# Stick-breaking heads: the strict mask moves from a TensorE matmul to a VectorE minimum behind the exponential

## The reference

```python
z = jnp.einsum('bqhd,bkhd->bhqk', qb, k, preferred_element_type=jnp.float32) * scale
q_pos = i * BLOCK + jnp.arange(BLOCK)
before = key_pos[None, :] < q_pos[:, None]
log_1m_beta = jnp.where(before, jax.nn.log_sigmoid(-z), 0.0)
tail = lax.cumsum(log_1m_beta, axis=3, reverse=True) - log_1m_beta
a = jnp.where(before, jnp.exp(jax.nn.log_sigmoid(z) + tail), 0.0).astype(v.dtype)
return jnp.einsum('bhqk,bkhd->bqhd', a, v)
```

## Time and profile before

| | before |
|---|---|
| median of three runs | 1734.01 us (1733.11 to 1734.31) |
| the profiled execution | 1734.41 us |
| its span, first to last instruction | 1732.6 us |
| TensorE busy | 1704.3 us |
| VectorE busy | 1107.1 us |
| ScalarE busy | 854.7 us |
| GpSimd busy | 142.0 us |
| mean granted TensorE clock | 0.997 |

### The profile page before, as it was taken

One profiled execution on the slowest core, in us unless ns is written; L12 is line 12 of the kernel. 1 busy time (PEld: TensorE's weight loads), 2 busy tenths in 40 slices (PEclk: granted clock), 3 DMA queues, 4 the chain that ended last, 5 costly groups with the idle time before them and its releaser, 6 DMA issues.

```text
span 1732.6 us, 21793 instructions
## 1 busy us (share of the span) xinstructions
PE 1704.3 (98%) x8585; PEld 1437.6 (83%) x8585; DVE 1107.1 (64%) x1498; ACT 854.7 (49%) x1203; POOL 142.0 (8%) x140
## 2 busy tenths in 40 slices
PE   9999999999999999999999999999999999999997
PEld 6888888888898888888888888888888988888886
DVE  8887887775566534364587777877754665344545
ACT  7576666665355414131466755666644554232223
POOL 0111211111100000000001111111111000000000
PEclk9999999999999999999999999999999999999999
DMA  4121121222432222222321211122224122222222
GB/s 149 67 73 59 60 74 62 77 75 80 138 118 74 97 98 97 98 98 97 119 82 65 76 61 61 61 74 74 74 85 164 68 98 97 98 97 98 97 98 73
DMA packets 47495, 152.09 MB, mean 88 GB/s; under 512 B 5153, under 2 KB 9633, under 8 KB 47394
## 3 DMA queue, kind: packets, MB, share of 16 engines
q1 hardware_dynamic: 45664, 147.42, 24.5%
q10 hardware_dynamic: 1730, 3.28, 0.5%
HBM read 146.49 MB, written 4.19 MB: 87 GB/s over the span
## 4 chain that ended last, share of the span: by engine, by line
PE 83%; issue 7%; DVE 6%; ACT 3%; POOL 1%; DMA 1%; DVEq 0%; SPq 0%; ACTq 0%; POOLq 0%
PE bank L579 77%; PE bank L584 3%; PE bank L834 1%; PE bank L885 1%; POOL mix L2303 1%; ACT w_hi L1039 1%; DVE w_lo L1582 0%; DVE h_lo L1617 0%; DVE hf L1629 0%; PE bank L588 0%; DMA x<-in_x 0%; PE bank L687 0%; DVE x L1638 0%; DVE fb L1828 0%; ACT dn L1096 0%
## 5 line engine op out<-in xcount | busy, mean ns | idle before, releaser
L579 PE MATMUL bank<-h_hi,w_hi 128*128 128x512 f32 (+1 forms) x1224 | 477.7, 390 | 4.6 <-DVE h_lo L1617 2.4
L579 PE MATMUL bank<-h_hi,w_lo 128*128 128x512 f32 (+1 forms) x1224 | 472.3, 386 | 0.0
L579 PE MATMUL bank<-h_lo,w_hi 128*128 128x512 f32 (+1 forms) x1224 | 472.3, 386 | 0.0
L1039 ACT ACTIVATE w_hi<-raw 128x1024 fp32r<-128x1024 f32 (+2 forms) x269 | 271.0, 1013 | 220.0 <-DMA raw<-in_w 219.6
L1582 DVE TENSOR_TENSOR w_lo<-raw,w_hi 128x1024 fp32r<-128x1024 f32 (+2 forms) x269 | 316.8, 1181 | 63.3 <-ACT w_hi L1039 56.9
L579 PEld LDWEIGHTS bank<-h_hi,w_hi 128*128 128x128 f32 x1224 | 230.4, 188 | 54.8 <-issue 5.7
L579 PEld LDWEIGHTS bank<-h_hi,w_lo 128*128 128x128 f32 x1224 | 230.3, 188 | 46.9
L579 PEld LDWEIGHTS bank<-h_lo,w_hi 128*128 128x128 f32 x1224 | 230.5, 188 | 45.2 <-issue 1.7
L579 PE MATMUL bank<-u_hi,w_hi 128*128 128x512 f32 (+1 forms) x560 | 208.0, 371 | 0.0
L579 PE MATMUL bank<-u_hi,w_lo 128*128 128x512 f32 (+1 forms) x560 | 207.7, 371 | 0.0
L579 PE MATMUL bank<-u_lo,w_hi 128*128 128x512 f32 (+1 forms) x560 | 207.7, 371 | 0.0
(11 more groups left out here) (264 smaller groups left out, 2747.3 us busy)
## 6 DMA issues: line engine op xcount, KB each, us to landing
raw<-in_w SPq DMA_DIRECT2D x251, 512.0 KB, 3.2
x<-in_x SPq DMA_DIRECT2D x16, 256.0 KB, 3.3
side_raw<-in_w SPq DMA_DIRECT2D x6, 512.0 KB, 4.8
x_spill<-x ACTq DMA_DIRECT2D x8, 256.0 KB, 2.5
x<-x_spill SPq DMA_DIRECT2D x8, 256.0 KB, 3.2
out_y<-x SPq DMA_DIRECT2D x8, 256.0 KB, 2.1
raw<-in_w SPq DMA_DIRECT2D x8, 192.0 KB, 2.4
raw<-in_w SPq DMA_DIRECT2D x8, 128.0 KB, 2.3
```

The source lines that it names most:

```text
L579: mm = pe.matmul(o, s, m, start=start and i == 0 and j == 0, stop=last and i == n - 1 and j == 2, skip_group_check=True)
L1039: act.activation(chunk_in(gc, w_hi, side_hi)[:, 0:w], chunk_in(gc, raw, side_raw)[:, 0:w], ACT.Copy)\
```

## The change

TensorE no longer adds the mask in `stick_tail`; the last matmul of each piece releases the exponential. Behind the exponentials of a head VectorE takes, in two instructions of 128 x 256, the minimum of the four diagonal blocks with a new table `tri_most`, which is 2^127 where the mask holds and 0 elsewhere (`stick_masked`). `stick_probs_hi` waits for both. ScalarE's split of the chunk moves from behind `stick_probs_hi(h)` to ahead of it. `tri01` is now made from `tri_most` by a scale; GpSimd's wait for it is taken once a layer, not once a head.

```diff
-                    def masked(b):
-                        causal_mask(*stick[h % 2][b], b, MASK_STRICT).then_inc(tail_full.sem, 1)
-
...
-                    less(0, P, 3 * P, NEG_ONE, later[:, 0:3 * P])
-                    masked(0)
-                    less(1, P, 2 * P, NEG_ONE, later[:, 4 * P:6 * P])
-                    masked(1)
+                    less(0, P, 3 * P, NEG_ONE, later[:, 0:3 * P]).then_inc(tail_full.sem, 1)
+                    less(1, P, 2 * P, NEG_ONE, later[:, 4 * P:6 * P]).then_inc(tail_full.sem, 1)
                     if h % 2:
                         pe.wait_ge(*a_exp(3 * h))
                     own(3)
-                    less(2, P, P, NEG_ONE, later[:, 3 * P:4 * P])
-                    masked(2)
+                    less(2, P, P, NEG_ONE, later[:, 3 * P:4 * P]).then_inc(tail_full.sem, 1)
...
                 def stick_probs_hi(h):
                     act.wait_ge(*a_exp(3 * h + 3))
+                    act.wait_ge(*a_mask(2 * h + 2))
                     act.wait_ge(*pv_full(2 * HEADS + h))
...
-                act.activation(tri01[:, :], cst_f[:, TRI01 * P:(TRI01 + 1) * P], ACT.Copy).then_inc(const_set, 1)
+                act.activation(tri_most[:, :], cst_f[:, TRI_MOST * P:(TRI_MOST + 1) * P], ACT.Copy).then_inc(const_set, 1)
+                act.activation(tri01[:, :], cst_f[:, TRI_MOST * P:(TRI_MOST + 1) * P], ACT.Copy, scale=1.0 / MOST)\
+                    .then_inc(const_set, 1)
...
                         stick_probs(h)
+                        split((C["stick_vt", p + 1] if more else C["gate", 2, 2]) + 2)
                         stick_probs_hi(h)
-                        split((C["stick_vt", p + 1] if more else C["gate", 2, 2]) + 2)
...
+                def stick_masked(h):
+
+                    b = fb[h % 2]
+                    dve.wait_ge(const_set, 3)
+                    dve.wait_ge(*a_exp(3 * h + 3))
+                    most = tri_most[:, :].unsqueeze(1).broadcast_to([P, 2, P])
+                    for two in (b[:, 0:2 * SEQ].rearrange("p (a c) -> p a c", a=2)[:, :, 0:P],
+                                b[:, 7 * P:9 * P].rearrange("p (a c) -> p a c", a=2)):
+                        dve.tensor_tensor(two, two, most, ALU.min).then_inc(a_mask.sem, 1)
...
                         stick_lo(h + 1)
                         if p:
                             stick_out(p - 1)
+                        stick_masked(h)
                         if more:
                             stick_in_low(p + 1, 1)
                         probs_lo(2 * HEADS + h, fb[0][:, :], p_hi[:, :], p_lo[:, :])
...
                             split(C["gate", 2, 2] + 2)
                             gate_in(2, 2)
+                        stick_masked(h + 1)
                         stick_sum(h)
```

More of the change, by code:

```diff
@@ L121 @@
 VECS = V_SINK + HEADS
-IDENT, SWAP, NEG_TRI, NEG_ONE, ONE, MASK_CAUSAL, MASK_PREV, MASK_STRICT, NEG_PART, TRI01 = range(10)
-N_CONST = 10 * P
+IDENT, SWAP, NEG_TRI, NEG_ONE, ONE, MASK_CAUSAL, MASK_PREV, NEG_PART, TRI_MOST = range(9)
+N_CONST = 9 * P
 TRIG = 4 * 4
@@ L128 @@
 BIG = 1e30
+MOST = 2.0 ** 127
 TWO_PI = float(2 * np.pi)
@@ L143 @@
 CAUSAL_COLS, BANDED_COLS = 1280, 896
+DIAGONAL = (0, 512, 896, 1024)
 def side_by_side():
@@ L194, in sem @@
             return ctx.enter_context(nc.semaphore(name))
-        tri01 = place("tri01", [P, P], F32)
+        tri_most, tri01 = (place(n, [P, P], F32) for n in ("tri_most", "tri01"))
         vec_all = place("vec_all", [P, DEPTH * VECS + TRIG], F32)
@@ L206, in trunk @@
         tab = place("tab", [P, 4, SEQ], F32)
-        cst = place("cst", [P, 9, P], F32R)
+        cst = place("cst", [P, 8, P], F32R)
         rstd_x = place("rstd_x", [P, SEQ], F32)
@@ L421, in trunk @@
         a_exp = signal("a_exp", 24)
+        a_mask = signal("a_masked", 16)
         sbo_part = signal("sb_o_part", 8)
@@ L1295, in _ @@
                 act.wait_ge(warmed, 1)
-                act.activation(cst[:, :, :], cst_f[:, 0:9 * P].rearrange("p (a c) -> p a c", a=9), ACT.Copy)\
+                act.activation(cst[:, :, :], cst_f[:, 0:8 * P].rearrange("p (a c) -> p a c", a=8), ACT.Copy)\
                    .then_inc(const_set, 1)
-                act.activation(tri01[:, :], cst_f[:, TRI01 * P:(TRI01 + 1) * P], ACT.Copy).then_inc(const_set, 1)
+                act.activation(tri_most[:, :], cst_f[:, TRI_MOST * P:(TRI_MOST + 1) * P], ACT.Copy).then_inc(const_set, 1)
+                act.activation(tri01[:, :], cst_f[:, TRI_MOST * P:(TRI_MOST + 1) * P], ACT.Copy, scale=1.0 / MOST)\
+                    .then_inc(const_set, 1)
                 table_sin(2, QPE, 2, slice(HEAD, P))
@@ L2323, in _ @@
                         band_maximum(n)
+                    pool.wait_ge(const_set, 3)
                     for h in range(HEADS):
@@ L2328, in _ @@
                             mix_in(1, h - 1)
-                        pool.wait_ge(const_set, 2)
                         pool.wait_ge(*z_max(3 * h + 3))
-                        for off in (0, 512, 896, 1024):
+                        for off in DIAGONAL:
                             to = fb[h % 2][:, off:off + P]
@@ L2345, in constants @@
     mats = [p == c, swap == c, -(p >= c).astype(np.float32), -np.ones((P, P)), np.ones((P, P)),
-            -BIG * (p > c), -BIG * (p <= c), -BIG * (p >= c), np.full((P, P), -1.0 / P), p < c]
+            -BIG * (p > c), -BIG * (p <= c), np.full((P, P), -1.0 / P), MOST * (p < c)]
     const = np.concatenate([np.asarray(m, np.float32) for m in mats], axis=1)
```

## The result

The changed kernel took 1747.42 us in the median of four runs (1743.97 to 1749.84), beside 1733.59 us before (1733.11 to 1734.31): ratio 1.0077, 95% interval 1.0063 to 1.0092, slower by 13.8 us. The forecast was slower by 9.5 us, 1743.5, with a range of 1740.5 to 1749.5. The profiled execution took 1746.67 us with a span of 1744.9, 12.3 us more than the 1732.6 before.

A forecast was written before the change was run, and what follows sets the result against it. TensorE, busy 98% of the span, was taken as the bound, waiting for p_lo at stick_values(2p). Added waits of 4.75 us a layer, 9.5 in two, on the profiled 1734.41 gave 1743.9, or 1743.5 as a median; range 1740.5 to 1749.5.

The forecast's parts named there:

- part 3: At stick_values(2p), minimums queued behind stick_lo and stick_out delay p_hi, p_lo and the values: 4.75 us a layer, 9.5 in two.
- part 2: On VectorE, two added minimums a head take 0.42 us each, 0.76 us together with overlap; bounds 0.48 and 1.30.
- part 1: In TensorE's tails, 48 removed mask matmuls save 0.24 us a head, 3.8 us in all, waited away at stick_values(2p).
- part 4: ScalarE's split ahead of p_hi costs nothing; VectorE's extra 0.76 us before gate(1,2p+1) costs nothing, with 0.7 us of cover.
- The likeliest case: The whole kernel takes 1743.5 us with no fall of the clock; chance 0.60 within the size bounds.
- Rival (A): TensorE's clock falls behind the longer holes, 1.6 us each: two falls give 1746.7, all six 1753.1; chance 0.25.
- its own row at 9.2 us: TensorE did 0.07 us of work from 9.20 to 11.50 us; from 12.50 the granted clock is 0.52.
- (B): At stick_values(2p), VectorE is not in the way and TensorE keeps its 3.8 us: 1730.2 us; chance 0.05.
- (C): VectorE falls behind after p_lo, with minimums of 0.69 us and waits before gate(1,2p+1): 1750.2 us; chance 0.05.
- (D): On VectorE, minimums cost the floor, 0.28 less a pair, 2.2 us in all: 1741.3 us; included in the 0.60.

The follow-up runs named there:

- first: The kernel before without its 48 mask matmuls and with nothing in their place: 1733.48 us, ratio 0.9999.
- second: The kernel before with all mask matmuls kept, plus the minimums, their wait and the moved split: 1746.39 us, ratio 1.0071.
- third: The changed kernel with stick_masked(h) moved one instruction earlier on VectorE, ahead of stick_out(p-1): 1743.15 us, ratio 1.0055.
- fifth experiment: The changed kernel with ScalarE's split moved back behind p_hi: 1747.29 us, ratio 1.0090.

## Why the prediction was right or wrong

**The chain at stick_values (part 3): right.** Predicted were 1.08, 1.51, 1.50 and 0.66 us for the four pairs; measured 1.12, 1.57, 1.56 and 0.58, together 4.83 against 4.75. Adding the minimums with the masks kept, and moving them by one instruction, showed that their place is the cause.

**The minimums (part 2): right.** 418 ns in the median of 32 and 0.76 us for a pair of them, as taken from the row of 128 x 256. The prediction gave 0.84 us as the price by the Trainium skill, "VectorE: DVE Perf Modes", section "The DRAIN you can't avoid". That left out the section's exception, that an instruction which isn't held starts earlier; the trace shows such an overlap, 0.08 us in a pair.

**The masks (part 1): the saving was waited away, as said, but its size was wrong.** A tail went from 1.97 to 1.61 us, 0.36 a head, not 0.24. The step that failed is the pricing of each mask from its own start to the next. The loads of stationary weights show why. In the kernel before, tail of head 2 (start, us, engine):

```profile
303.40 0.19 PEld L584 LDWEIGHTS bank<-sp_lo,cst 128*128 128x128 f32 x1
303.52 0.19 PEld L584 LDWEIGHTS bank<-later,cst 128*128 128x128 f32 x1
303.64 0.19 PEld L584 LDWEIGHTS bank<-cst 128*128 128x128 f32 x1
303.75 0.19 PEld L579 LDWEIGHTS bank<-h_hi,w_hi 128*128 128x128 f32 x1
```

The first line is the load for a matmul of 256 columns, the second and third are for matmuls of 128. In this stretch the loads start 0.11 to 0.12 us apart whatever the width. A matmul of 128 columns can start 0.06 us ahead of the next, but three loads of 0.12 make 0.36, which is what the tail lost. That the loads are the cause is read from these rows; no run varied them. In this kernel the error changed mainly the length of the holes, 2.80 and 2.10 us where 2.6 and 2.0 were said.

**The split and the rest (part 4): right.** The split cost nothing in either place, and gate(1,2p+1) waited no longer than before. Not foreseen: in pair 0 the projection behind the first tail came early enough to wait 0.30 us for VectorE to empty its bank, inside the shadow of the hole:

```profile
259.42 0.47 PE L582 MATMUL bank<-h_hi,w_hi 128*128 128x512 f32 x1 [0.30 <-DVE tmp L1661]
```

**The likeliest case: wrong by the clock.** Rival (A) was named and priced, two falls of 1.6 us and 1746.7 us. It happened, at 1.6 and 1.5 us in the profile, and the median is 1747.42. The forecast took no fall as likeliest, at 0.60 against 0.25, though its own row at 9.2 us showed a fall behind a stop of 2.3 us, and two of the holes it predicted were longer than that and four nearly as long. The 1743.5 of part 3's sum is near the fastest run (1743.97) and the kernel with its holes filled (1743.49), so it is the time without falls. The median lay within the range because that left room for three falls; the chain alone would not have brought it to 1747.42, and one of the four runs (1749.84) is above the range.

**Rivals (B), (C) and (D)** did not come: no pair's values started straight behind the tail, no gate waited longer, and the minimums were not shorter than taken.

## What to carry to other kernels

Work taken from the busiest engine can be worth nothing until the next wait of that engine is moved too, as 48 matmuls were here: ask at which wait the saving arrives, and what has to be earlier there. When that wait is for another engine, an instruction added to the other engine costs what its place in the queue makes it cost, not only its length: 0.76 us of minimums cost 1.5 us a pair here. And before giving up an edit that only lengthened a wait, look for independent work that the waiting engine can do in it: one projection in front of the values turned a loss of 13.8 us into a gain of 9.1, of which 4.6 come without the change and 4.5 with it.

## What the runs showed of the hardware

TensorE's clock fell to 1.2 GHz behind waits shorter than I had reckoned with. In the stick heads of the profiles of the kernel before and of the five with longer holes (the changed kernel and the first, second, third and fifth experiment), a fall, to a granted clock of 0.50, stood behind 6 of 8 holes of 2.5 to 2.8 us, 2 of 8 of 2.1 us, 1 of 2 of 1.7 us, and none of the 8 of 1.4 to 1.5 us, the 2 of 1.34 us or any shorter one. The same hole of the same kernel had a fall in one layer and none in the other, for which I have no cause, and the changed kernel's time is spread over its runs by 5.9 us, against 0.5 us with the holes filled. Each fall cost 1.5 to 1.6 us. The Trainium skill, "TensorE: Matmul & The Clock Gate", section "HAM oscillation — how this bites in real kernels", describes such losses for waits for transfers; here the wait was for VectorE.

In a tail's short matmuls with changing weights, the loads start 0.11 to 0.12 us apart, whether the matmul has 128 or 256 columns, and taking out two of 128 and one of 256 shortened the tail by 0.36 us.
